# Deferred weight pieces, regrouped expert tail, a merged norm and wide up products in a two-block network

## What is computed

```python
def _squared_relu_mlp(h, w_up, w_down):      # 1024 -> 4096 -> 1024
    u = jax.nn.relu(h @ w_up)
    return (u * u) @ w_down
```

## Time and profile before

| what | value |
|---|---|
| device time, median of 3 runs | 2691.22 us (2679.55 to 2700.61) |
| profiled execution: device time | 2695.73 us |
| profiled execution: span | 2693.9 us |
| mean granted TensorE clock | 0.967 of full |
| TensorE matmul busy | 2492.3 us, 93% of the span |
| VectorE busy | 1673.1 us, 62% |
| ScalarE busy | 1318.6 us, 49% |
| DMA | 539.89 MB, mean 200 GB/s |

### The profile page before, as it was taken

How to read it: one execution, slowest core, us unless ns; L and a number is a source line. 1 busy time by engine, 2 the same in 40 slices (tenths; PEclk the granted TensorE clock), 3 DMA queues, 4 the chain that set the end, 5 groups by cost and what they waited for, 6 DMA issues and landing times.

```text
span 2693.9 us, 32883 instructions
## 1 busy us (share of the span) xinstructions
PE 2492.3 (93%) x13426; PEld 2133.6 (79%) x13426; DVE 1673.1 (62%) x1486; ACT 1318.6 (49%) x1794; POOL 92.0 (3%) x121
## 2 busy tenths in 40 slices
PE   4988999898888999998999999899997999999999
PEld 3877777787777777777977998689986899987998
DVE  5757788786657877775644555645556555644554
ACT  3444777433553756653344444544445444444443
POOL 1000000000100000000000000100001000000000
PEclk9997999998997999999999999999999999999999
DMA  8713999983622979883553595335543355553553
GB/s 279 245 52 137 338 340 332 336 306 131 219 79 96 330 265 319 285 303 119 191 176 131 183 252 198 129 109 189 187 150 117 120 188 188 185 192 124 184 188 125
DMA packets 231301, 539.89 MB, mean 200 GB/s; under 512 B 21072, under 2 KB 29808, under 8 KB 231152
## 3 DMA queue, kind: packets, MB, share of 16 engines
q1 hardware_dynamic: 208992, 471.82, 50.9%
q0 software_dynamic: 15520, 59.77, 6.3%
q10 hardware_dynamic: 6640, 6.20, 1.2%
HBM read 533.54 MB, written 4.19 MB: 200 GB/s over the span
## 4 chain that ended last, share of the span: by engine, by line
PE 62%; DVE 16%; DMA 10%; ACT 6%; issue 3%; POOL 1%; SPq 1%; ACTq 0%; DVEq 0%
DVE w_low L2107 7%; PE pair L974 6%; PE pair L966 6%; PE pair L968 5%; PE Y L1084 5%; PE Y L1086 5%; PE Y L1094 5%; PE pair L1001 4%; PE pair L1002 4%; PE pair L1007 4%; DMA raw<-in_exp_w_down 4%; ACT w_high L1670 3%; DMA raw<-in_exp_w_gate 3%; PE Y L1377 2%; PE Y L1379 2%
## 5 line engine op out<-in xcount | busy, mean ns | idle before, releaser
L2107 DVE TENSOR_TENSOR w_low<-raw,w_high 128x2048 fp32r<-128x2048 f32 (+3 forms) x456 | 1021.8, 2247 | 614.1 <-ACT w_high L1670 609.6
L1670 ACT ACTIVATE w_high<-raw 128x1024 fp32r<-128x1024 f32 (+3 forms) x912 | 911.3, 1038 | 775.3 <-PE Y L1094 201.3
L966 PE MATMUL pair<-hT_high,w_high 128*128 128x256 f32 x1280 | 311.9, 284 | 0.4
L968 PE MATMUL pair<-hT_low,w_high 128*128 128x256 f32 x1280 | 311.1, 283 | 0.0
L1001 PE MATMUL pair<-w_high,hT_high 128*128 128x512 f32 (+1 forms) x612 | 240.7, 394 | 10.4 <-DVE hT_low L2163 5.2
L966 PEld LDWEIGHTS pair<-hT_high,w_high 128*128 128x128 f32 x1280 | 245.9, 192 | 2.9 <-issue 1.9
L968 PEld LDWEIGHTS pair<-hT_low,w_high 128*128 128x128 f32 x1280 | 246.0, 192 | 0.9
L1002 PE MATMUL pair<-w_high,hT_low 128*128 128x512 f32 (+1 forms) x612 | 239.4, 392 | 0.0
L1086 PE MATMUL Y<-w_high,gated_low 128*128 128x512 f32 x528 | 205.8, 390 | 0.0
L1084 PE MATMUL Y<-w_high,gated_high 128*128 128x512 f32 x528 | 205.7, 390 | 0.0
L1377 PE MATMUL Y<-w_high,gated_high 128*128 128x512 f32 x320 | 134.5, 420 | 41.3 <-DVE gated_low L2430 36.6
(11 more groups left out here) (367 smaller groups left out, 3741.5 us busy)
## 6 DMA issues: line engine op xcount, KB each, us to landing
raw<-in_exp_w_gate SPq DMA_DIRECT2D x128, 512.0 KB, 4.8
raw<-in_exp_w_up SPq DMA_DIRECT2D x128, 512.0 KB, 5.1
raw<-in_exp_w_down SPq DMA_DIRECT2D x128, 512.0 KB, 4.9
raw<-in_w_up SPq DMA_DIRECT2D x128, 512.0 KB, 4.6
raw<-in_w_down SPq DMA_DIRECT2D x128, 512.0 KB, 4.5
work<-in_w_mod POOLq DMA_DIRECT2D x48, 1024.0 KB, 7.6
raw<-in_ret_w_in SPq DMA_DIRECT2D x96, 512.0 KB, 4.8
raw<-in_ret_w_out SPq DMA_DIRECT2D x32, 512.0 KB, 4.1
```

What stands on the lines that cost most here:

```text
L966: nc.tensor.matmul(ps[:, f, :], high[:, k, f * P:(f + 1) * P], hT_high[:, kk, :], start=(kk == 0 and f % 2 == 0), stop=False)
L968: nc.tensor.matmul(ps[:, f, :], high[:, k, f * P:(f + 1) * P], hT_low[:, kk, :], start=False, stop=False)
L1670: nc.scalar.activation(w_high[:, s % HIGH, part], raw[:, s % RAW, part], ACT.Copy).then_inc(high_ready, 1)
L2107: V.tensor_tensor(w_low[:, s % HIGH, 0:n], part, w_high[:, s % HIGH, 0:n].bitcast(F32), ALU.subtract).then_inc(low_ready, 1)
```

## The change

1. **Deferred pieces.** On the last projection of each attention ScalarE and VectorE no longer make the last piece's parts before the attention; the `feed` at its end makes them. The sine moves behind the first attention.
2. **Experts.** The 20 halves are dealt 4, 5, 5, 6; the first of the five places is used only with more than 4 halves; at the last expert the place behind its products is dropped and the rest is done after the low parts of the last windows. GpSimd starts each of the first three loads behind one of the pieces of the first heavy expert. `down` waits for each window only before that window's matmuls. After the last expert the products are turned before the gate row is spread.
3. **Merged norm.** The first block's final norm is no longer ahead of the retention norm: TensorE turns the unscaled `x`, the gain is the product of both gains, `x` is scaled behind that on VectorE, and the kept factor is the product of both inverse roots.
4. **Wide up products.** From step 2 of each MLP on, `hT_high` and `hT_low` are one tile and move together, 512 columns for one stationary block; the two halves of the result are added later. An up product is then 32 matmuls of 512 columns and 32 of 256 and takes both PSUM pairs.

```diff
+WIDE_FROM = 2
@@ make_plan
-        p.moe0.halves[at] = halves[5 * i:5 * i + 5]
+    for at, (first, last) in zip(range(LIGHT * PER_GROUP, EXPERTS), ((0, 4), (4, 9), (9, 14), (14, 20))):
+        p.moe0.halves[at] = halves[first:last]
@@ gpsimd
-            wait_piece(pool, 2 * plan.moe0.up[LIGHT * PER_GROUP - 1] + 1)
-            load_mods(STAGES["moe0"])
+            for i, (n, h) in enumerate((n, h) for n in STAGES["moe0"] for h in range(2)):
+                if i < SLOTS_OF["moe0"]:
+                    wait_piece(pool, 2 * plan.moe0.gate[LIGHT * PER_GROUP] + i)
+                load_mod(n, h)
@@ tensor: new
+            def wide_product(uses):
+                for j in range(2):
...
+                    for i, each in enumerate(uses):
+                        ps = pair(each)[:, :].rearrange("p (f n) -> p f n", f=2)
...
+                        for q in range(2):
...
+                            for f in range(2):
...
+                                    nc.tensor.matmul(ps[:, f, :], high[:, k, fs], hT[:, :, kk, :], start=(kk == 0), stop=False)
+                    wait_low(s)
+                    for i, each in enumerate(uses):
...
+                                last = nc.tensor.matmul(ps[:, f, 0:S], low[:, k, fs], hT_high[:, kk, :],
+                                                        start=False, stop=(kk == KD - 1))
+                        if i == 0 and j == 1:
+                            last.then_inc(first_pair_done, 1)
+                    last.then_inc(piece_done, 1)
@@ norm_by_block
-                pe.wait_ge(updated, TB * n.after)
+                pe.wait_ge(updated, TB * n.turned_after)
@@ experts on tensor: down
-                    for v, _ in units:
-                        wait_emptied(pe, m.unit_use[v])
...
                         for v, w in units:
+                            if h == 0:
+                                wait_emptied(pe, m.unit_use[v])
...
+                turn(last_units)
                 gate_rows([unit_gate(m, v) for v, _ in last_units], MOD[m.nth] + G2).then_inc(gate_filled, 1)
-                turn(last_units)
@@ mlp on scalar
+                            lower = pair(each)[:, :].rearrange("p (f n) -> p f n", f=2)[:, :, S:2 * S]
+                            nc.scalar.activation(act[:, at % 2, 2 * i:2 * i + 2], lower, ACT.Copy).then_inc(lower_copied, 1)
@@ retention on scalar
+                if r is plan.ret0:
+                    norm_highs(r.norm, gain_b)
+                    final_squares()
+                    feed(r.norm.feed)
+                    norm_squares(r.norm, tokpair(qT_area))
@@ by_token on scalar
-                    feed(2 * use.chunk + 5)
+                    if use is not proj[-1]:
+                        feed(2 * use.chunk + 5)
@@ experts on vector
                     if heavy:
-                        one_half()
+                        if len(halves) > 4:
+                            one_half()
...
-                    one_half()
+                    if at < EXPERTS - 1:
+                        one_half()
...
                 gated_lows(m.units[EXPERTS - 1])
+                while halves:
+                    one_half()
@@ mlp on vector
-                    feed(2 * use.chunk + 4)
+                    feed(2 * use.chunk + 2)
...
+                    feed(2 * use.chunk + 4)
...
+                            ve.wait_ge(lower_copied, 2 * (m.first_up + j) + i + 1)
+                            empties(each, V.tensor_tensor(both, upper, both, ALU.add))
...
+                        V.scalar_tensor_tensor(prod, act[:, at % 2], 0.0, act[:, at % 2],
+                                               ALU.max, ALU.mult).then_inc(product_ready, 1)
@@ retention on vector
+                norm(r.norm, gain_b if r is plan.ret0 else cols[:, N1_G + layer * KD:N1_G + (layer + 1) * KD])
+                if r is plan.ret0:
+                    final_norm()
...
+                    link(V.tensor_tensor(of_tokens, of_tokens, rs[:, plan.final_stat % 2, 0:TB], ALU.mult))
@@ vector, ahead of the first block's latent attention and of MoBA and differential attention
-            feed(2 * plan.uq[2].chunk + 5)
+            feed(2 * plan.uq[2].chunk + 4)
-                feed(2 * a.proj[5].chunk + 5)
+                feed(2 * a.proj[5].chunk + 4)
```

113 lines of the change are left out of this document (82 added, 31 removed).

## The result

The changed kernel takes 2657.60 us (median of 4 runs, 2646.69 to 2661.38), the kernel before 2690.72 us (median of 4 runs, 2679.55 to 2700.61). The medians differ by 33.1 us; the ratio is 0.986, 95% interval 0.9833 to 0.9887: 1.4% faster. The forecast was 2654 us. The profiled execution took 2658.39 us with a span of 2656.6 us, 37.3 us less than before; the sum of the forecast was 36.9 us.

A forecast was written before the change was run, and what follows sets the result against it. TensorE bounds the MLPs; elsewhere it idles behind VectorE, ScalarE or loads. Terms 10.1 + 8.9 + 7.3 + 4.1 + 1.7 + 4.8 = 36.9 us gave 2654 us against the median; own range 2644 to 2664, widened to 2638 to 2676.

The forecast's parts named there:

- Wide products, 10.1 us: Four MLPs: one 512-column matmul replaces two of 256, saving 0.42 us in each of 24 up products, 10.1 us.
- both PSUM pairs must be free again after the down product alone: MLPs: the down product gives 10.9 us of cover; copy, additions and one rounding need about 4 us.
- Deferred pieces, 8.9 us: Four attentions: deferring the last piece nets 2.0 in the first, -0.1 latent, 3.4 MoBA, 3.6 differential; together 8.9 us.
- 4.3, 3.4 and 3.6: Starts of first, MoBA and differential attention: keys can be copied sooner without the piece, by these us.
- net of -0.1: Latent attention: one low part fewer before the first score block gives 2.2 us, but 2.3 us come back at its end.
- the 2.0 of the first attention: First attention: 4.3 us gained at the start, 2.3 us come back at the end, net 2.0 us.
- Heavy experts, 7.3 us: Layer 0: later loads gain 3.5 us, one half fewer before the products 3.11, waiting per window 0.7; sum 7.3 us.
- VectorE is the bound until the next down product: Heavy experts of layer 0: the next down product waits 2.40 us for VectorE, whose chain gains 3.5 of 5.5 us.
- That the stall moves: Rival, heavy experts: if a half waits for its load on VectorE, 7.3 and part of 4.1 us go; 2664 us, chance 0.14.
- Last expert of layer 0, 4.1 us: Without the 3.11 us half before the low parts, down starts sooner; a shorter wait saves perhaps 1 us more; 4.1 us.
- Last expert of layer 1, 1.7 us: Turned first, products wait about 1.2 us for VectorE and the gate row fills the rest of 3.14 us; 1.7 us.
- Merged norm, 4.8 us: Join of the blocks: TensorE may turn at 1257.4, when x is final, instead of 1262.19; 4.8 us, later scaling hidden.

The follow-up runs named there:

- undisturbed ones: Profiles with the changed kernel's heavy experts (narrow up products, no deferral, separate norm): 135.7 us each from first turn to last, wait at second turn 0.27 us.
- the loads spread out: Changed kernel with the first three loads of condition rows behind pieces 1, 3 and 5 of the first heavy expert, not 0, 1 and 2; span 2652.6 us.
- the repair that moves the low part: Changed kernel with the last expert's next-piece low part behind those of its windows, run together with a bias-row repair; span 2648.6 us.
- two other profiles of the same layer 1: Changed kernel with narrow up products, and with separate final norm: 366.8 and 367.6 us in that part of layer 1; spans 2658.5 and 2662.3 us.
- the first two repairs: Changed kernel with bias rows spread behind the first MLP's second up product and the last expert's extra low part behind its windows' low parts; span 2648.6 us.

## Why the prediction was right

**Wide products, 10.1 us:** the step that each pair saves 0.0131 us was right: 0.42 us forecast for a product, 0.41 measured. The rows of 512 columns held for a split operand. By the rule of the Trainium skill ("TensorE: Matmul & The Clock Gate", section "Back-to-back issue gap"), the columns over 2.4 GHz plus 2.5 ns, a pair would save 2.5 ns, so, as an estimate from the page, 0.08 us a product; the pairs saved 12.7 ns each, and the trace does not agree. The prediction took this rule for the spacing of a stream; that section calls it the gap of an isolated matmul and gives 131 ns at 512 columns for a stream of weight loads and matmuls, which the 0.229 us measured here does not bear out either. What failed is "both PSUM pairs must be free again after the down product alone". In the first MLP the bias rows hold one of the pairs just then, and their copy comes late. 5 to 7 us came, not 10.1.

**Deferred pieces, 8.9 us:** the steps at the starts held to 0.3 us: waits shorter by 4.3 (2.7 for the piece, 1.6 for the sine), 3.3 and 3.5 us against 4.3, 3.4 and 3.6. That MoBA and differential attention give nothing back is shown by three profiles without deferral against eleven with it (4.2 and 3.7 us). In the latent attention the low part delayed not the first scores, which wait for ScalarE, but the masking behind them, and 2.4 to 2.7 us came there for the 2.2; its net of -0.1 and the 2.0 of the first attention fit the stages, but can't be tested against 3 us of scatter.

**Heavy experts, 7.3 us:** 5.3 us in the first pair of profiles, 4.6 in the means of the two pairs, 7.9 in the mean of all nine profiles with these loads and halves, and up to 12 in the undisturbed ones. "VectorE is the bound until the next down product" was right. That the stall moves was a rival (chance 0.14). In a third of the profiles a part of it came true, though not as "a half waits for its load on VectorE": the gate weights of the next expert land behind the loads, and 4.3 to 4.7 us stand at the next turn. The rival's form itself showed only with the loads spread out.

**Last expert of layer 0, 4.1 us:** 5.2 us, of which the place of the halves is 2.3. The gate row's place brought nothing.

**Last expert of layer 1, 1.7 us:** 0. The step "turned first, the products wait about 1.2 us for VectorE and the gate row fills the rest" left out the low part between the products and the windows' low parts in VectorE's program (and its own terms, 3.14 less 1.2, give 1.9). From the start of the last up product to that of the last down product it took 16.9 us before, 16.2 with the change, in either order of the gate row, and 14.8 with the repair that moves the low part, which brought 1.4 us. The 0.7 us that came without it fit the wait per window. The new wait of 2.0 us before the last but one down product, from the half that slid behind the products, took more than that.

**Merged norm, 4.8 us:** 5.4 us, nothing given back. The forecast counted from the final `x`; the first turns start on its first half, at 1232.92, which may be the rest.

**Not forecast:** 5 to 6 us in the light experts of layer 0, whose cause is open, and 6.6 us in layer 1 ahead of its last experts, where two other profiles of the same layer 1 show none of it. In the first pair of profiles these two bring 13.6 us, and all other stages 23.7 us in place of 36.9. That the total of 37.3 us met the sum is therefore partly luck; the mechanisms of the steps were right in the main.

## What to carry to other kernels

Before two accumulators are used at once, list every other tenant of them, small ones too, and where in the program of the engine that empties them the emptying stands: a copy of 0.35 us held a product up for 2 to 3 us because it stood behind a low part that had itself to wait. An engine's order is worth changing only if that engine ends last; a gate row moved on TensorE brought nothing that could be read, one low part moved on VectorE 1.4 us. When a condition is written for one stage (more than four halves), look where else it holds: in layer 1 it cost a wait of 2 us. And profile the kernel before twice ahead of reading terms of 2 us: here, steady stages repeat to 0.1 us, stages with short waits or a full DMA to 2 to 4 us.

## What the runs showed of the hardware

- The same short wait in the same place may or may not be followed by a lower clock. Behind the wait of 2.77 us in the first retention the 10 us had a granted clock of 0.67 or 1.00. Behind a wait of 2 us before the second heavy down product it was 0.66 in one kernel and 1.00 in another whose program there is the same:

```profile
518.00:528.00 10.00, 9.67 (x42) 8.27 (x41) 7.84 (x9) 2.00 (x2) 1.50 (x2) 0.66 0.94 335
```
```profile
517.00:527.00 10.00, 9.67 (x56) 8.37 (x55) 7.59 (x9) 2.52 (x3) 1.50 (x2) 1.00 0.96 347
```

  The first is the kernel with the first two repairs, the second the one without deferral; from this down product to the last turn they took 102.05 and 98.83 us.
- A full mean clock is not time: products of no use raised it from 0.968 and 0.971 to 0.980 for nothing that could be measured.
- A moving operand taken from two places in one matmul of 512 columns started every 0.229 us, like one that lies in one place.
